# A macaron layer on one core: order of the opening's weight splits and the form of the last norm

## The chip, the cores and the metric

The kernel runs on one core of a Trainium2 chip. The metric is device microseconds of one execution; before, three runs took 982.69 to 983.95 us, median 983.18.

## What is computed

One residual layer on 512 tokens of width 1024, all in float32. `x` is normed, then three sub-layers follow, each of the form `x <- LayerNorm(ALPHA * x + w * gate * f(x * (1 + scale) + shift))`, with f a SwiGLU feed-forward net (D_FF = 2816), then a mixer (latent attention beside pooled channel groups), then a second SwiGLU net. Shift, scale and gate come from `silu(c) @ w_ada + b_ada`.

```python
x = _layernorm(x, ln_in_g, ln_in_b)
mod = (c_act @ w_ada[l] + b_ada[l]).reshape(B, N_SUBLAYERS, 3, D)
h = x * (1.0 + scale[:, 0, None, :]) + shift[:, 0, None, :]
y = _swiglu(h, ffn1_w_in[l], ffn1_w_out[l])
...
x = _layernorm(ALPHA * x + 0.5 * gate[:, 2, None, :] * y, post_ln_g[l, 2], post_ln_b[l, 2])

def _layernorm(x, g, b):
    mu = jnp.mean(xf, axis=-1, keepdims=True)
    var = jnp.mean(jnp.square(xf - mu), axis=-1, keepdims=True)
    return (xf - mu) * lax.rsqrt(var + LN_EPS) * g + b
```

## The kernel before

Activations are kept transposed: `x` is eight tiles (KD = 8) of 128 features by 512 tokens. A sum over features therefore runs over partitions and is made on TensorE with a matrix of ones. Weights come in units of 128x1024 (eight 128x128 blocks, one for each tile of h). For accuracy each factor is held as a high and a low part (`w_hi`, `w_lo`, `h_hi`, `h_lo`), and a product is three matmuls, w_hi with h_hi, w_hi with h_lo, w_lo with h_hi (`mm3`, L551 to L553). ScalarE writes a unit's high part (`act_hi`, L927), VectorE its low part (`dve_lo`, L935), from one of three slots `raw` that SyncE fills; the load of unit n waits until unit n - 3 is split (`s_lo`). Each engine runs its own hand-written program in order; semaphores join them.

**Opening.** SyncE loads the columns, x, c, and then in turn units and pairs of w_ada tiles (`ada_first`, a ring of 12). VectorE takes the input norm's statistics, and then for each k of 0 to 7: two products of w_ada with c (L1472) that give scale and shift of tile k (`first_columns`, L1475), the split of unit k while k < 6 (EARLY), and the low part of h of tile k - 1 (`first_low`, L1463). ScalarE normalises the token-major x (`normal`, L1051: four first halves ahead of the loop, the second halves in steps k = 0 and 1), TensorE transposes it back, ScalarE applies gain and offset (`affine`, L1056), makes h and its high part (L1069, L1072), and then splits unit k + 1. TensorE (`early_units`) fills six banks, one for each of units 0 to 5. In step k it adds the low part of tile k - 1 to the banks of units 0 to k - 1 (L614), catches up on unit k with all earlier tiles (L551 to L553), and adds the two high products of tile k to units 0 to k (L622, L623). Behind tile 7 it runs unit by unit from L627 on and then goes straight into the rest of the first net.

**Last norm.** TensorE closes the mean (L641, bank 6) and the mean square (L645, bank 7). ScalarE squares the mean (L945) and copies it (L946), VectorE forms the variance (L1262), ScalarE takes Ln (L950) and Exp (L952) of it, and VectorE refines that by one Newton step of three instructions (L1269, L1271, L1273). VectorE centres tiles 0 to 2 early, and then goes through the tiles in order, centring (L1276) and scaling (L1285). Gain and offset are applied by ScalarE (L1199; tiles 0, 2, 3, 5, 7) and GpSimd (L1771; tiles 1, 4, 6), and SyncE stores the tiles in order (L540), each behind its own wait.

## Time and profile before

| | |
|---|---|
| median of three runs | 983.18 us |
| the profiled execution | 983.47 us |
| its span, first to last instruction | 981.7 us |
| TensorE matmuls busy | 944.1 us, 96% |
| VectorE busy | 508.1 us, 52% |
| ScalarE busy | 373.2 us, 38% |
| GpSimd busy | 242.8 us, 25% |
| mean granted TensorE clock | 0.984 of full speed |
| moved by DMA | 127.20 MB, mean 130 GB/s |

Times within the trace are counted from the first instruction. In the page a slice is 24.5 us; all slices of TensorE but the first and the last show 90% or more. Engines are named PE (TensorE), DVE (VectorE), ACT (ScalarE), POOL (GpSimd) and SP (SyncE) in the rows; PEld are weight loads and SPq the DMA issues of SyncE. L12 is line 12 of the kernel.

### The profile page before, as it was taken

Reading aid. Unit: us, or ns where it says so; the run is one execution under the profiler, and the core shown is the slowest. Engines: PE = TensorE matmul, PEld = TensorE weight load, DVE = VectorE, ACT = ScalarE, POOL = GpSimd, SP = SyncE. Lnnn points to the kernel's source line nnn. Section 1 sums busy time; section 2 is a strip of 40 time slices with the busy share of each in tenths; the row PEclk is TensorE's granted clock in tenths of the full one; section 3 lists DMA queues with packets and bytes.
Section 4 is the critical chain, followed back from the end, with each engine's and each line's share of the span. In section 5 each row is a group of like instructions: output and inputs, shape, how many; then the busy total and the mean of one; then the engine's idle time right before and its main releaser. Section 6 shows DMA issues by size and latency. Waiting matters only on the chain.

```text
span 981.7 us, 10623 instructions
## 1 busy us (share of the span) xinstructions
PE 944.1 (96%) x4130; PEld 759.8 (77%) x4130; DVE 508.1 (52%) x718; ACT 373.2 (38%) x546; POOL 242.8 (25%) x209
## 2 busy tenths in 40 slices
PE   4999999999999999999999999999999999999992
PEld 3788888888888887787766786888888888888881
DVE  5956767454465764767655477722322232234225
ACT  4743232333222332765584447532333233222213
POOL 0021111111106221328934363611111111053110
PEclk8899999999999999999999999999999999999997
DMA  9836565656553753113501112223232323222202
GB/s 367 334 111 207 178 208 182 205 179 209 184 181 128 228 180 129 54 65 107 139 34 44 43 65 82 101 98 107 86 108 86 108 86 101 79 95 91 90 17 85
DMA packets 37474, 127.20 MB, mean 130 GB/s; under 512 B 4016, under 2 KB 4144, under 8 KB 37424
## 3 DMA queue, kind: packets, MB, share of 16 engines
q1 hardware_dynamic: 37424, 126.52, 38.4%
q8 instruction: 33, 0.54, 0.2%
q14 instruction: 17, 0.14, 0.0%
HBM read 123.36 MB, written 2.10 MB: 128 GB/s over the span
## 4 chain that ended last, share of the span: by engine, by line
PE 92%; DVE 3%; ACT 2%; issue 1%; POOL 1%; DMA 0%; SPq 0%; ACTq 0%; DVEq 0%; POOLq 0%
PE bank L551 28%; PE bank L553 28%; PE bank L552 28%; PE bank L856 2%; PE bank L833 1%; PE bank L659 1%; PE bank L623 1%; PE bank L622 1%; PE bank L614 1%; DVE x L1285 1%; DVE bn L1435 0%; PE bank L844 0%; PE bank L588 0%; DMA x<-xT 0%; POOL q_sum L1713 0%
## 5 line engine op out<-in xcount | busy, mean ns | idle before, releaser
L935 DVE TENSOR_TENSOR w_lo<-raw,w_hi 128x1024 fp32r<-128x1024 f32 x159 | 216.4, 1367 | 298.6 <-ACT w_hi L927 298.2
L551 PE MATMUL bank<-h_hi,w_hi 128*128 128x512 f32 x730 | 286.6, 393 | 0.0
L553 PE MATMUL bank<-h_hi,w_lo 128*128 128x512 f32 x730 | 284.4, 390 | 0.0
L552 PE MATMUL bank<-h_lo,w_hi 128*128 128x512 f32 x730 | 284.4, 390 | 0.0
L927 ACT ACTIVATE w_hi<-raw 128x1024 fp32r<-128x1024 f32 x159 | 162.3, 1032 | 204.0 <-PE bank L553 203.0
L1663 POOL TENSOR_TENSOR a_lo<-act_t,a_hi 128x512 fp32r<-128x512 f32 x44 | 58.4, 1328 | 426.7 <-ACT a_hi L1011 426.7
L551 PEld LDWEIGHTS bank<-h_hi,w_hi 128*128 128x128 f32 x730 | 137.3, 188 | 28.9 <-issue 0.8
L553 PEld LDWEIGHTS bank<-h_hi,w_lo 128*128 128x128 f32 x730 | 137.2, 188 | 29.0
L552 PEld LDWEIGHTS bank<-h_lo,w_hi 128*128 128x128 f32 x730 | 137.4, 188 | 28.6 <-issue 0.5
L551 PE MATMUL bank<-a_hi,w_hi 128*128 128x512 f32 x352 | 138.6, 394 | 0.0
L553 PE MATMUL bank<-a_hi,w_lo 128*128 128x512 f32 x352 | 137.0, 389 | 0.0
L552 PE MATMUL bank<-a_lo,w_hi 128*128 128x512 f32 x352 | 136.9, 389 | 0.0
L552 PEld LDWEIGHTS bank<-a_lo,w_hi 128*128 128x128 f32 x352 | 66.1, 188 | 14.7 <-issue 1.0
L551 PEld LDWEIGHTS bank<-a_hi,w_hi 128*128 128x128 f32 x352 | 66.1, 188 | 14.4 <-issue 1.0
L553 PEld LDWEIGHTS bank<-a_hi,w_lo 128*128 128x128 f32 x352 | 66.1, 188 | 13.8
L1217 DVE SCALAR_TENSOR_TENSOR var<-ada_ring,c_act 128x1024 bf16<-128x1024 f32 x56 | 72.5, 1296 | 3.6 <-DMA ada_ring<-ada_w 3.6
L1011 ACT ACTIVATE a_hi<-act_t 128x512 fp32r<-128x512 f32 x44 | 27.8, 632 | 110.0 <-DVE act_t L1325 103.3
L993 ACT ACTIVATE sq<-x 128x512 f32<-128x512 f32 x21 | 13.2, 628 | 108.3 <-DVE x L1313 108.2
L1313 DVE SCALAR_TENSOR_TENSOR x<-bank,gate,x 128x512 f32<-128x512 f32 x16 | 12.0, 750 | 77.3 <-PE bank L553 72.0
L1681 POOL TENSOR_TENSOR s_sum<-s_sum,x 128x512 f32<-128x512 f32 x15 | 23.0, 1534 | 98.1 <-DVE x L1313 93.9
L1020 ACT ACTIVATE act_t<-bank 128x512 f32<-128x512 f32 x42 | 25.0, 596 | 45.4 <-PE bank L553 45.4
L1672 POOL TENSOR_TENSOR x<-x,shift 128x512 f32<-128x512 f32 x16 | 25.9, 1654 | 57.6 <-DVE shift L1310 57.6
(252 smaller groups left out, 999.1 us busy)
## 6 DMA issues: line engine op xcount, KB each, us to landing
raw<-wunits SPq DMA_DIRECT2D x145, 512.0 KB, 3.2
ada_ring<-ada_w SPq DMA_DIRECT2D x56, 512.0 KB, 4.4
ada_first<-ada_w SPq DMA_DIRECT2D x16, 512.0 KB, 9.0
raw<-wunits SPq DMA_DIRECT2D x16, 384.0 KB, 2.8
x<-xT SPq DMA_DIRECT2D x4, 512.0 KB, 5.6
outT<-x SPq DMA_DIRECT2D x8, 256.0 KB, 2.0
K<-k_rope SPq DMA_DIRECT2D x2, 512.0 KB, 8.8
c_act<-c_rows SPq DMA_DIRECT2D x1, 512.0 KB, 7.5
```

Of the source, the lines that this page charges most:

```text
L551: mm(out, lh, rh, start=first, stop=False)
L552: mm(out, lh, rl, start=False, stop=False)
L553: return mm(out, ll, rh, start=False, stop=last)
L856: last = mm(bank[PV_BANK][:, j * P:], v, PT[hd % 2][:, j, j * P:], start=j == 0, stop=j == QB - 1)
L927: nc.scalar.activation(parts(n, 0, width)[0], raw[:, slot, 0:width], ACT.Copy)\
L935: nc.vector.tensor_tensor(lo, raw[:, slot, 0:width], hi.bitcast(F32), SUB).then_inc(s_lo, 1)
L1011: fn(a_hi[:, t - 1, :], act_t[:, (t - 1) % 2, :], ACT.Copy).then_inc(s_ah[f], 1)
L1020: fn(act_t[:, t % 2, :], bank[up_bank(f, t)][:], ACT.Silu).then_inc(s_silu[f], 1)
L1217: stt(junk, slot_ap, 1.0, c_act[:], MUL, MUL, accum_out=mod[:, t:t + 1])\
L1663: tt(a_lo[:, t, :], act_t[:, t % 2, :], a_hi[:, t, :].bitcast(F32), SUB)\
L1672: tt(x[:, m, :], x[:, m, :], shift[:], SUB).then_inc(s_xs[p], 1)
L1681: tt(s_sum[:], s_sum[:], x[:, m, :], ADD).then_inc(s_acc[p], 1)
```

## The change

In the opening each engine's split of a unit moves one step ahead: VectorE splits units 0 and 1 in step 0 and unit k + 1 in step k, and it does so behind `first_low(k - 1)`, no longer ahead of it. ScalarE splits unit 1 between the first four `normal` passes and the first `affine`, and unit k + 2 in step k. TensorE starts with two banks for tile 0 and catches up on unit k + 1 in step k; for unit 2's bank it waits for two second-half `normal` passes. SyncE issues units 1 and 2 right behind the first pair of w_ada tiles, and units 3, 4 and 5, each with its wait for a split, behind the pairs of steps 1, 2 and 3.

In the last norm the inverse root is one function of ScalarE, `Abs_reciprocal_sqrt`, read straight from the bank of the variance and loaded ahead of time by `preload`; the Newton step stays, with banks 0 and 1 as scratch. The tiles are centred on three engines: tile 0 on VectorE, tiles 1 to 3 on GpSimd by adding `shift` = -mean, tiles 4 to 7 on TensorE as an identity matmul of x plus one of `shift` into banks 2 to 5. VectorE scales seven tiles, GpSimd tile 3. ScalarE applies gain and offset to four tiles, GpSimd to three, VectorE to tile 7. The stores follow the new order.

```diff
@@ -74,7 +74,12 @@
 AFFINE_STEP = 4
-POOL_LAST = (1, 4, 6)
+LAST_POOL = (1, 2, 3)
+LAST_PE = (4, 5, 6, 7)
+LAST_SCALED = (4, 5, 0, 1, 2, 6, 7)
+LAST_ACT_OUT = (4, 5, 0, 2)
+LAST_POOL_OUT = (1, 6)
+LAST_STORED = (4, 5, 3, 0, 1, 2, 6, 7)
@@ -321,6 +326,7 @@
         def y_bank(p, m):
             return bank[OUT_BANK[m] if p == 2 else Y0 + m % 2]
+        ROOT_BANK, CENTRED_BANK = (0, 1), (2, 3, 4, 5)
@@ -411,6 +417,7 @@
         s_pf, s_mc = sem("pool_finished"), sem("mean_copied")
+        s_pc = sem("centred_by_matmul")
@@ -494,16 +501,16 @@
             for k in range(KD):
-                if k < RAWS:
-                    unit(k)
+                if k == 0:
+                    unit(0)
...
                         .then_inc(s_ada1[a % FIRST_RING], 16)
-                if RAWS <= k < EARLY:
-                    unit(k)
+                for n in range(1, RAWS) if k == 0 else range(k + 2, min(k + 3, EARLY)):
+                    unit(n)
@@ -532,11 +539,15 @@
                 unit(n)
-            for m in range(KD):
-                if m in POOL_LAST:
-                    sp.wait_ge(s_pf, POOL_LAST.index(m) + 1)
+            for m in LAST_STORED:
+                if m in LAST_ACT_OUT:
+                    sp.wait_ge(s_hh[3], LAST_ACT_OUT.index(m) + 1)
+                elif m == LAST_POOL[-1]:
+                    sp.wait_ge(s_pf, len(LAST_POOL) + 2)
+                elif m in LAST_POOL_OUT:
+                    sp.wait_ge(s_pf, len(LAST_POOL) + 3 + LAST_POOL_OUT.index(m))
                 else:
-                    sp.wait_ge(s_hh[3], m + 1 - sum(n < m for n in POOL_LAST))
+                    sp.wait_ge(s_nx[3], len(LAST_SCALED) + 1)
@@ -610,14 +621,18 @@
                         pe.wait_ge(s_hl[0], k)
-                        for j in range(min(k, EARLY)):
+                        for j in range(min(k + 1, EARLY)):
                             mm(bank[j][:], w(j, (k - 1) * P)[0], h_lo[:, k - 1, :], start=False, stop=False)
-                    if k < EARLY:
-                        pe.wait_ge(s_lo, k + 1)
+                    if k == 1:
+                        pe.wait_ge(s_xna, QB + 2)
+                    if 0 < k < EARLY - 1:
+                        pe.wait_ge(s_lo, k + 2)
                         for kk in range(k):
-                            mm3(bank[k][:], w(k, kk * P), h(kk), kk == 0, False)
+                            mm3(bank[k + 1][:], w(k + 1, kk * P), h(kk), kk == 0, False)
                     pe.wait_ge(s_hh[0], k + 1)
-                    for j in range(min(k + 1, EARLY)):
+                    for j in range(min(k + 2, EARLY)):
+                        if k == 0:
+                            pe.wait_ge(s_lo, j + 1)
@@ -715,6 +730,14 @@
                     down_tile(base, per, p, rhs, k_last, m, ready)
+            def last_centred():
+                pe.wait_ge(s_mc, 3)
+                for b, m in zip(CENTRED_BANK, LAST_PE):
+                    if m != LAST_PE[0]:
+                        mm(bank[b][:], ident, x[:, m, :], start=True, stop=False)
+                    mm(bank[b][:], ident, shift[:], start=False, stop=True).then_inc(s_pc, 1)
             def ffn(base, f, p, a_hi, a_lo):
@@ -732,7 +755,9 @@
                 if f == 1:
+                    mm(bank[CENTRED_BANK[0]][:], ident, x[:, LAST_PE[0], :], start=True, stop=False)
                     stats_end(p + 1)
+                    last_centred()
@@ -951,6 +976,16 @@
                 fn(y0[:], y0[:], ACT.Exp, scale=-0.5).then_inc(s_rq[p], 1)
+            def last_root():
+                act.wait_ge(s_st[3], 1)
+                fn(tmp[:], bank[MEAN[3]][:], ACT.Square).then_inc(s_rq[3], 1)
+                fn(shift[:], bank[MEAN[3]][:], ACT.Copy, scale=-1.0).then_inc(s_mc, 1)
+                act.wait_ge(s_rv[3], 1)
+                fn(y0[:], bank[SQR[3]][:], ACT.Abs_reciprocal_sqrt).then_inc(s_rq[3], 1)
+                act.wait_ge(s_rv[3], 4)
+                fn(bank[SQR[3]][:], rstd[:], ACT.Copy).then_inc(s_rq[3], 1)
             def preload(n, func):
@@ -1037,11 +1072,14 @@
                             act_hi(act, n)
-                preload(2 + f, ACT.Ln)
+                preload(2 + f, ACT.Abs_reciprocal_sqrt if f else ACT.Ln)
...
                 square(p, KD - 1)
-                root(p, 1, MX + LEAD if f == 0 else None)
+                if f == 0:
+                    root(p, 1, MX + LEAD)
+                else:
+                    last_root()
@@ -1059,6 +1097,7 @@
                 normal(t, 0)
+            act_hi(act, 1)
@@ -1070,8 +1109,8 @@
                 fn(h_hi[:, k, :], act_t[:, k % 2, :], ACT.Copy).then_inc(s_hh[0], 1)
-                if k + 1 < EARLY:
-                    act_hi(act, k + 1)
+                if k + 2 < EARLY:
+                    act_hi(act, k + 2)
@@ -1192,10 +1231,8 @@
             ffn(F2, 1, 3, a_hi2)
-            for m in range(KD):
-                if m in POOL_LAST:
-                    continue
-                act.wait_ge(s_nx[3], m + 1)
+            for m in LAST_ACT_OUT:
+                act.wait_ge(s_nx[3], LAST_SCALED.index(m) + 1)
@@ -1271,6 +1308,40 @@
                 stt(bank[SQR[p]][:], tmp[:], 1.5, y0[:], ADD, MUL).then_inc(s_rv[p], 1)
+            def last_norm():
+                mean, square = bank[MEAN[3]], bank[SQR[3]]
+                z, w = (bank[b] for b in ROOT_BANK)
+                dve.wait_ge(s_st[3], 2)
+                dve.wait_ge(s_rq[3], 1)
+                stt(square[:], square[:], SUM_EPS, tmp[:], ADD, SUB).then_inc(s_rv[3], 1)
+                dve.wait_ge(s_mc, 3)
+                centre(3, 0, mean)
+                dve.wait_ge(s_rv[3], 1)
+                dve.wait_ge(s_rq[3], 2)
+                tt(z[:], square[:], y0[:], MUL).then_inc(s_rv[3], 1)
+                dve.wait_ge(s_rv[3], 2)
+                stt(w[:], z[:], -0.5, y0[:], MUL, MUL).then_inc(s_rv[3], 1)
+                dve.wait_ge(s_rv[3], 3)
+                stt(rstd[:], w[:], 1.5, y0[:], ADD, MUL).then_inc(s_rv[3], 1)
+                dve.wait_ge(s_rv[3], 4)
+                for m in LAST_SCALED:
+                    if m == 0:
+                        dve.wait_ge(s_cen[3], 1)
+                        dve.wait_ge(s_rq[3], 3)
+                        scaled = tt(x[:, m, :], x[:, m, :], square[:], MUL)
+                    elif m in LAST_POOL:
+                        dve.wait_ge(s_pf, LAST_POOL.index(m) + 1)
+                        scaled = tt(x[:, m, :], x[:, m, :], square[:], MUL)
+                    else:
+                        dve.wait_ge(s_pc, LAST_PE.index(m) + 1)
+                        scaled = tt(x[:, m, :], bank[CENTRED_BANK[LAST_PE.index(m)]][:], rstd[:], MUL)
+                    scaled.then_inc(s_nx[3], 1)
+                m, c = LAST_SCALED[-1], 3 * KD + LAST_SCALED[-1]
+                dve.wait_ge(s_nx[3], len(LAST_SCALED))
+                ts(x[:, m, :], x[:, m, :], cols[:, C_LNG + c:C_LNG + c + 1],
+                   cols[:, C_LNB + c:C_LNB + c + 1], MUL, ADD).then_inc(s_nx[3], 1)
             def centre(p, m, mean):
@@ -1425,8 +1496,11 @@
                     plain_low(p, KD - 1)
-                root(p, 2, MX + LEAD if f == 0 else None)
-                normalise(p, MX if f == 0 else None)
+                if f == 0:
+                    root(p, 2, MX + LEAD)
+                    normalise(p, MX)
+                else:
+                    last_norm()
@@ -1473,10 +1547,10 @@
                 tt(first_col[:, k, :], mod_pair[:, k, :], bias_pair[:, k, :], ADD).then_inc(s_fc, 1)
-                if k < EARLY:
-                    dve_lo(dve, k)
...
                     first_low(k - 1)
+                for n in range(2) if k == 0 else range(k + 1, min(k + 2, EARLY)):
+                    dve_lo(dve, n)
@@ -1765,9 +1839,19 @@
             ffn(1, 3, a_hi2, a_lo2)
-            for m in POOL_LAST:
+            pool.wait_ge(s_mc, 3)
+            for m in LAST_POOL:
+                tt(x[:, m, :], x[:, m, :], shift[:], ADD).then_inc(s_pf, 1)
+            pool.wait_ge(s_pf, len(LAST_POOL))
+            pool.wait_ge(s_rv[3], 4)
+            m = LAST_POOL[-1]
+            tt(x[:, m, :], x[:, m, :], rstd[:], MUL).then_inc(s_pf, 1)
+            for m in (LAST_POOL[-1], *LAST_POOL_OUT):
                 c = 3 * KD + m
-                pool.wait_ge(s_nx[3], m + 1)
+                if m == LAST_POOL[-1]:
+                    pool.wait_ge(s_pf, len(LAST_POOL) + 1)
+                else:
+                    pool.wait_ge(s_nx[3], LAST_SCALED.index(m) + 1)
```

## Rows read from the trace of the kernel before

**Rows 1.** The page, part 1: busy us (share of the span) x instructions.

```profile
PE 944.1 (96%) x4130; PEld 759.8 (77%) x4130; DVE 508.1 (52%) x718; ACT 373.2 (38%) x546; POOL 242.8 (25%) x209
```

**Rows 2.** The chain of waits, 20 to 34: start us, us, what.

```profile
25.65 0.69 DVE h_lo L1463
27.18 0.43 PE bank L551
32.81 0.23 PE bank L553
```

**Rows 3.** Timeline of TensorE, end of the early units: start us, us, what.

```profile
63.38 0.39 PE L553 MATMUL bank<-h_hi,w_lo_early 128*128 128x512 f32 x1
```

**Rows 4.** Windows: length, busy us of each engine, granted clock, DMA share, GB/s.

```profile
24.00:26.00 2.00, 0.86 (x2) 0.14 (x1) 1.50 (x2) 2.00 (x4) 0.00 (x0) 0.50 1.01 414
32.00:33.00 1.00, 1.00 (x5) 0.81 (x4) 0.96 (x3) 1.00 (x2) 0.00 (x0) 0.77 0.89 320
```

**Rows 5.** The chain of waits, 960 to the end.

```profile
963.54 0.87 PE bank L645 x2
964.44 0.70 DVE var L1262
965.16 0.63 ACT y L950
965.81 1.28 ACT L952
967.11 0.64 ACT y L952
969.96 1.88 DVE x L1285 x3
978.48 0.81 ACT x L1199
```

**Rows 6.** Timelines of VectorE, ScalarE and TensorE in the opening.

```profile
19.03 1.22 DVE L935 TENSOR_TENSOR w_lo<-raw,w_hi 128x1024 fp32r<-128x1024 f32 x1
24.50 1.22 DVE L935 TENSOR_TENSOR w_lo<-raw,w_hi 128x1024 fp32r<-128x1024 f32 x1 [1.77 <-ACT w_hi L927]
28.81 1.23 DVE L935 TENSOR_TENSOR w_lo<-raw,w_hi 128x1024 fp32r<-128x1024 f32 x1
20.53 1.63 ACT L1056 ACTIVATE x<-bank,cols 128x512 f32<-128x512 f32 x2 [1.21 <-PE bank L588]
23.43 1.04 ACT L927 ACTIVATE w_hi<-raw 128x1024 fp32r<-128x1024 f32 x1
27.20 0.63 ACT L1072 ACTIVATE h_hi<-act_t 128x512 fp32r<-128x512 f32 x1
28.69 1.43 ACT L1051 ACTIVATE x_tok<-bank,tshift,trstd 128x512 f32<-128x512 f32 x2
26.39 0.80 PE L614 MATMUL bank<-h_lo,w_hi 128*128 128x512 f32 x1 [1.52 <-DVE h_lo L1463]
```

**Rows 7.** SyncE's timeline; DMA issues of 0:9.6, of 25:28 (count, KB, us to landing).

```profile
20.28 0.33 SPq L488 DMA_DIRECT2D raw<-wunits  x1
20.65 0.91 SPq L503 DMA_DIRECT2D ada_first<-ada_w  x2
ada_first<-ada_w SPq DMA_DIRECT2D x8, 512.0 KB, 12.2
raw<-wunits SPq DMA_DIRECT2D x1, 512.0 KB, 3.7
```

**Rows 8.** Timelines of TensorE and of SyncE at the end.

```profile
962.42 1.12 PE L641 MATMUL bank<-x,ones_d 128*128 128x512 f32 x2 [0.84 <-DVE x L1313]
979.32 0.33 SPq L540 DMA_DIRECT2D outT<-x  x1
```

**Rows 9.** GpSimd: L1672 by itself (ns min/median/max); L1771 among the groups.

```profile
L1672 POOL TENSOR_TENSOR x<-x,shift x16: 1290/1298/2271, 302.1 to 882.3; 128x512 f32<-128x512 f32 x16
L1771 POOL TENSOR_SCALAR x<-x,cols 128x512 f32<-128x512 f32 x3 | 2.3, 768 | 27.4 <-DVE x L1285 27.4
```

## The prediction

> **What bounds the kernel now.** I read the page's busy shares first: TensorE works 944.1 of 981.7 us [rows 1], so all that an edit can save outside TensorE's own work is in the 37.6 us in which it waits, and the chain of waits says where those are. Two stretches matter. In the opening TensorE stands still until the first low part of h (the `first_low` of tile 0, VectorE) is there at 26.34, and from 26.39 on it has no gap up to the last product of the early units, which ends at 63.77 [rows 2, 3]. It also starts that stretch at the lower clock: the granted clock is 0.50 in 24 to 26 and reaches 1.00 at about 32.5 (0.77 as a mean of 32 to 33) [rows 4], after work that had run unbroken since 26.39, and the step from one product to the next falls from 0.43 to 0.23 us [rows 2]. At the end TensorE is done at 964.4 and the last 17.3 us are a chain that it has no part in: variance, Ln, table load, Exp, three Newton steps, 13 passes over 128x512 on VectorE, one affine pass on ScalarE, one store [rows 5].
>
> **The opening, part by part.** In the order of before, unit 1 is split only behind h of tile 0: ScalarE makes `w_hi` of it at 23.43, VectorE waits 1.77 us for that, splits from 24.50, and only then comes `first_low(0)` at 25.65, for which TensorE waits 1.52 us [rows 6]. The change puts ScalarE's part (`act_hi(1)`, 1.04 us) into the idle 1.21 us ahead of the first affine pass at 20.53 [rows 6], so it costs ScalarE nothing; the cover is thin (0.17 us), and what it lacks shifts h of tile 0 by that much. VectorE's part follows unit 0 directly: 19.03 + 1.14 = 20.17, then to 21.3, with its operand ready at about 20.3. `first_low(0)` then stands behind two products of w_ada (2.3 us) alone and ends at about 24.4 instead of 26.3, and each later step of VectorE, whose period is 4.31 us (24.50 to 28.81) [rows 6], is some 0.8 to 1.9 us earlier.
>
> TensorE gets two banks' work for tile 0 (4 products instead of 2) from 23.67, at 0.43 us each to 25.5; then 2 low products to 26.4, 3 products that begin bank 2 (their `w_lo` is there at 25.6, the new wait for `s_xna` QB + 2 is over at 25.7, when the pair of normal passes ahead of the affine pass ends) to 27.7, and it meets h of tile 1 at 27.75, which ScalarE makes no earlier than before (27.20 + 0.53) [rows 6]. So it works on with about 0.1 us idle from 23.67. The number of products is the same 144 (6 units x 8 tiles x 3). Two prices bound the gain. If the clock rises when it did (32.5), before had 14 products done and after has 18: 4 x 0.23 = 0.9 us. If it rises up to 3 us earlier, as the unbroken work now begins 2.7 us earlier, the next hold is the wait for the second halves of x_tok at 30.0 (ScalarE 28.69 + 1.33 [rows 6], unchanged). There 15 products are done and 129 x 0.23 = 29.3 us are left, with four groups of transposes, each counted as two products (1.8): end 61.1. The same count for before from 32.5, 130 products and three groups, ends at 63.4. Gain 2.3. I take 1.9, nearer to the second end, since in before 6.1 us of unbroken work were enough, and 23.67 + 6.1 = 29.8. Later gates don't hold: `first_low(1)` at about 28.7, unit 3's `w_lo` at 29.9 and h of tile 2 at 32.05 stand against TensorE's need at 30.5, 31.2 and 32.6.
>
> SyncE's queue pays for this. Before, eight w_ada tiles were issued without a wait and unit 3 behind them at 20.28 [rows 7]. Now unit 3's wait for the first split (over at 20.2) stands ahead of tiles 4 to 15, and units 4 and 5 wait there too (21.3 and 25.6). The loads ahead of it, 6.4 MB, are in by about 18.4 at 414 GB/s [rows 4], so the DMA engines are idle for some 3 us that they were busy before. VectorE wants tiles 4 and 5 at 25.6 and 26.7. Issued at 20.7 and 21.1 into an empty queue and behind unit 3, with 3.7 us for a landing in 25 to 28 [rows 7] and 1.26 us more for each 0.52 MB, they land at about 24.7 and 26.0: 0.7 us of slack. Tiles 6 and 7 have 1.2. A miss of up to 1 us is taken up by the slack that TensorE's gates above show. Cost 0, bounds 0 to 1.
>
> **The end, part by part.** TensorE gets seven identity products behind the sums. The first (x of tile 4) lies in the 0.84 us in which it waits for the last residual; an f32 product takes 0.87 [rows 5, 8], so it may cost 0.1. The others begin when -mean is in `shift`, about 964.65, and give tiles 4, 5, 6 and 7 at 965.8, 967.5, 969.2 and 971.0 in banks, if the clock holds at 2.4 GHz. The variance stays as it is, 964.44 to 965.14. Then one ScalarE function for the root instead of Ln 0.63, load 1.28 and Exp 0.63 [rows 5]: the result is there at 965.8, not 967.75, 1.95 us saved. The three Newton steps have the same count and operands of the same kind: 965.8 + 3 x 0.73 = 968.0.
>
> Now VectorE has one centring pass (in the shade of the root), seven scalings and one affine pass, where it had five centrings and eight scalings from 969.96 to 978.45, 8.5 us. Scalings without a dependence follow each other at 0.60 (1.88 for three) [rows 5]: 968.0 + 6 x 0.6 + 0.7 = 972.3; the affine pass of tile 7 on VectorE has no row of its own shape here between 0.4 and 0.7 us (a pass from one SBUF tile against one from two); I take 0.5: 972.8. GpSimd: three centrings at 1.29 (its fastest and its middle row; 2.27 the slowest [rows 9]) from 964.7 to 968.5, scaling of tile 3 to 969.9, three affine passes at 0.77: tile 3 to 970.7, tile 1 (scaled at 970.4) to 971.5, tile 6 (scaled at 971.7) to 972.5. ScalarE: four affine passes of 0.81, the last (tile 2) to 971.9. The stores go out in the order 4, 5, 3, 0, 1, 2, 6, 7, each 0.33; the last at 972.95 in place of 979.32 [rows 8], and it takes 2.4 us to the end as now. End 975.3 against 981.7: 6.4 saved, less 0.1 for the product before the sums and 0.1 for stores that now follow each other closer. I take 6.2; the bounds are 5.2 (each hand-over 0.1 late, stores in a queue) and 6.6.
>
> **A rule on the load and one on the port.** The load of the table takes 1.28 us in the chain, and Exp begins 1.30 us after it began [rows 5]. The Trainium skill, ScalarE: Activation LUTs, section What ACT_TABLE_LOAD costs, gives 1.28 us and some 1.38 of draining on top, 2.66 in all; by that the end would save 1.4 us more. The trace has no such time between load and Exp, so the sum stays with 1.28. GpSimd's passes over x take 1.29 to 2.27 us [rows 9]; the long ones lie beside VectorE's splits, which read two SBUF tiles. The Trainium skill, SBUF — State Buffer, Reading the diagram, says that VectorE with two SBUF inputs or in a two-port mode and GpSimd lock each other out for whole instructions. All passes of VectorE in the new norm but the last take one operand from a bank, so by that rule 1.29 holds.
>
> **Sum.** 1.9 + 6.2 = 8.1. The profiled execution took 983.47 (span 981.7 and 1.8 around it): 975.4. It was 0.3 above the median of the three runs, 983.18, which would give 975.1; I say 975.2.
>
> **Rivals.** (1) Clock unchanged or loads late: TensorE keeps 1.2 GHz to 32.5, or waits about 1 us for w_ada tiles 4 and 5. For it: the gap at 24.86 was not the only thing ahead of the rise, and the slack of 0.7 us rests on a landing time in another load. Opening 0.9: 976.1. (2) GpSimd is slowed at the end. Its seven passes at 2.27 for those over two tiles: centrings end at 971.5, scaling 973.8, then three times 0.77 to 976.1, and the last store leaves at 976.8: the end saves 2.5, time 978.8. For it: such rows exist; against it: 0.77 for its affine pass while VectorE was scaling from a bank without a pause [rows 9]. (3) The change doesn't do what it says: the root function or the Square and Copy around it still draw a table load in the chain, because the set preloaded doesn't hold them all. 1.28 each, one or two: 976.5 to 977.8. Against it: in before Ln had been preloaded too, `root` ran a Square and a Copy behind that, and no load stands between the variance and Ln [rows 5]. (4) Slower than before: the refill of w_ada. VectorE takes 13 us from tile 5's landing to the split of unit 5 (three steps of 4.31), and TensorE has about 19.6 us of work behind that, so the opening ends at landing + 32.6. It decides from a landing at 31.2, when the opening gains nothing; to eat the end's 6.2 us too and 2 us more it must land at 39.4, 18 us after its issue. The longest middle value of a landing here is 12.2, in a full queue [rows 7], which would give 65.9 for the opening and 979.1 in all.
>
> **How the numbers follow.** Forecast 0.66 (974.2 to 976.0), rival 1 0.15, rival 2 0.07, rival 3 0.08, rival 4 0.01, and 0.03 for what I don't see. 0.2% is 2.0 us, about what a measurement tells from no change. All but rival 4 and the unseen lie over 5 us below before: faster 0.97, same 0.02, slower 0.01. The range leaves out rival 2, part of rival 3 and the rest: 974.1 to 977.4.
>
> **What would show it.** Right: TensorE without a gap over 0.3 us from 23.7; the clock at 1.00 before 30.5; the last early product ending at about 61.5 to 62; no table load behind the sums; the rstd bank or tile ready at 968.0, counted from a variance at 964.4; VectorE's last pass at about 8.4 us behind the variance; the span's end 10.9 us behind it (17.3 now). Wrong: VectorE waiting for ada_first over 1 us, GpSimd passes of 2 us in the last norm, stores that land over 3 us after issue, or a gap of TensorE between 64 and 962 that before didn't have.

## The result and the profile after

Four runs of the changed kernel took 976.36 to 978.24 us, median 976.99; four of the kernel before 982.69 to 984.07, median 983.57. The ratio is 0.9936 with a 95% interval of 0.9918 to 0.9953: 6.6 us faster, inside the range of the prediction, 1.8 us above its single value of 975.2. The profiled execution took 977.08 us, 6.4 less than that of before. Further down, each ratio is to runs of the kernel before that were made alongside, with medians of 983.55 to 984.01 us.

The page of the changed kernel: span, busy shares, and the granted clock in 40 slices.

```profile
span 975.3 us, 10654 instructions
PE 949.1 (97%) x4146; PEld 760.3 (78%) x4146; DVE 504.5 (52%) x711; ACT 370.7 (38%) x544; POOL 246.8 (25%) x213
PEclk8999999999999999999999999999999999999999
```

I cut both spans at two points, the start of the last early product and the start of the variance's instruction:

| | before | after | gain |
|---|---|---|---|
| first instruction to the last early product | 63.38 | 61.04 | 2.34 |
| from there to the variance (the middle) | 901.06 | 902.08 | -1.02 |
| variance to the end of the span (the tail) | 17.25 | 12.17 | 5.08 |
| span | 981.7 | 975.3 | 6.4 |

The opening, timelines of TensorE and then of VectorE (start us, us, what, idle before and its releaser), to be held against [rows 3, 6]:

```profile
23.46 0.50 PE L637 MATMUL bank<-h_hi,w_hi 128*128 128x512 f32 x1 [0.58 <-ACT h_hi L1111]
25.77 0.47 PE L562 MATMUL bank<-h_hi,w_hi 128*128 128x512 f32 x1 [0.49 <-ACT x_tok L1089]
27.77 0.50 PE L637 MATMUL bank<-h_hi,w_hi 128*128 128x512 f32 x1 [1.06 <-ACT h_hi L1111]
30.05 0.66 PE L599 MATMUL bank<-cols,x_tok 128*128 128x128 f32 x4 [0.63 <-ACT x_tok L1089]
61.04 0.39 PE L564 MATMUL bank<-h_hi,w_lo_early 128*128 128x512 f32 x1
23.81 0.68 DVE L1537 TENSOR_TENSOR h_lo<-act_t,h_hi 128x512 fp32r<-128x512 f32 x1
26.98 1.23 DVE L1546 SCALAR_TENSOR_TENSOR tmp<-ada_first,c_act 128x1024 bf16<-128x1024 f32 x1 [0.21 <-DMA ada_first<-ada_w]
```

`first_low(0)` starts at 23.81, no longer at 25.65, and TensorE has products of tile 0 up to 25.28. Behind them it waits three times: for a released bank (0.49), for h of tile 1 (1.06) and for the second halves of x_tok (0.63). The prediction had no gap over 0.3 us here. At the higher clock TensorE reaches these gates early; in the one profile of the new order in which the clock rose only at 26.8 the first two waits are missing. The granted clock stands behind them: as means of two windows, with busy times of PE, PEld, DVE, ACT and POOL, the clock, DMA share and GB/s, against 0.50 in 24 to 26 in [rows 4]:

```profile
20.00:24.00 4.00, 3.40 (x16) 2.57 (x15) 3.91 (x8) 3.63 (x6) 0.00 (x0) 0.70 0.72 256
24.00:26.00 2.00, 1.51 (x6) 0.74 (x5) 2.00 (x3) 2.00 (x4) 0.00 (x0) 1.00 0.92 291
```

It was up at 22.4, ten microseconds earlier than in before, while the 16 transposes of x_tok (19.25 to 22.9) still ran.

The end, from the chain of waits, to be held against [rows 5]:

```profile
963.12 0.71 DVE bank L1318
963.86 0.60 ACT y L985
964.56 0.71 DVE bank L1323
966.02 0.70 DVE rstd L1327
969.83 1.21 DVE x L1339 x2
971.06 0.55 DVE x L1343
```

One function of ScalarE stands between the variance and the Newton steps, with no table load. VectorE's last pass ends 8.5 us behind the start of the variance. GpSimd's part in its timeline: three centrings in 3.73 us, the scaling, two affine passes; the third affine pass follows at 970.53.

```profile
963.43 3.73 POOL L1844 TENSOR_TENSOR x<-x,shift 128x512 f32<-128x512 f32 x3 [16.46 <-ACT shift L983]
967.23 1.27 POOL L1848 TENSOR_TENSOR x<-x,rstd 128x512 f32<-128x512 f32 x1
968.61 1.52 POOL L1855 TENSOR_SCALAR x<-x,cols 128x512 f32<-128x512 f32 x2
```

### The profile page after: what moved, and what is told of

Same layout as the page of the kernel before. It is cut to its first block, busy times and chain, and to the rows that moved or that the text cites. A ratio compares the mean times of both kernels' runs of the same rounds, so it can differ in the third digit from the quotient of the medians.

```text
span 975.3 us, 10654 instructions
## 1 busy us (share of the span) xinstructions
PE 949.1 (97%) x4146; PEld 760.3 (78%) x4146; DVE 504.5 (52%) x711; ACT 370.7 (38%) x544; POOL 246.8 (25%) x213
## 4 chain that ended last, share of the span: by engine, by line
PE 91%; DVE 3%; ACT 3%; issue 1%; POOL 1%; DMA 1%; SPq 0%; ACTq 0%; DVEq 0%; POOLq 0%
PE bank L562 28%; PE bank L564 28%; PE bank L563 28%; PE bank L881 2%; PE bank L858 1%; PE bank L674 1%; PE bank L637 1%; PE bank L638 1%; DMA x<-xT 1%; PE bank L625 1%; ACT x_tok L1089 1%; PE bank L869 1%; DVE bn L1509 1%; DVE w_lo L960 0%; POOL q_sum L1787 0%
```

## Where the middle lost one microsecond

Matching TensorE's instructions of both traces one by one shows the same lead of 2.34 us from the opening up to 481 us, and of 1.3 us from 491 on; nothing changes after that. The place is the start of the attention, a place that the change doesn't touch. VectorE's and GpSimd's timelines of before:

```profile
487.29 1.23 DVE L935 TENSOR_TENSOR w_lo<-raw,w_hi 128x1024 fp32r<-128x1024 f32 x1
487.36 2.29 POOL L1749 TENSOR_TENSOR h_lo<-act_t,h_hi 128x512 fp32r<-128x512 f32 x1
```

and of after, with TensorE's instruction behind it:

```profile
485.06 2.36 DVE L960 TENSOR_TENSOR w_lo<-raw,w_hi 128x1024 fp32r<-128x1024 f32 x1
485.05 1.29 POOL L1823 TENSOR_TENSOR h_lo<-act_t,h_hi 128x512 fp32r<-128x512 f32 x1
489.13 0.70 PE L858 MATMUL bank<-K,Q 128*128 128x256 f32 x2 [0.66 <-ACT cq L1193]
```

The weight split on VectorE reads two SBUF tiles, and so does GpSimd's pass over h. In before the split started 0.07 us ahead and took 1.23 us, and GpSimd's pass took 2.29, stretched by the split. In after GpSimd's pass started 0.01 us ahead and kept its 1.29, and the split took 2.36. The split stands in VectorE's queue ahead of the next score's maximum, so ScalarE's exponential and TensorE's next scores come late. The Trainium skill, SBUF — State Buffer, Reading the diagram, states that the one of the two that starts first holds the shared port for its whole instruction; these four rows agree: the first keeps its time, and the second ends 1.14 us (before) and 1.08 us (after) behind the end of the first, 0.15 less than it takes by itself. My prediction used that rule for the last norm and not for what the whole shift of the timeline does to ties elsewhere.

## Experiments

**The opening alone.** The five pieces of the diff in SyncE's loop over k, `early_units`, ScalarE's and VectorE's opening; the last norm is that of before.

```diff
             for t in range(QB):
                 normal(t, 0)
+            act_hi(act, 1)
...
-                if k < EARLY:
-                    dve_lo(dve, k)
                 if k:
                     first_low(k - 1)
+                for n in range(2) if k == 0 else range(k + 1, min(k + 2, EARLY)):
+                    dve_lo(dve, n)
```

> Only the opening's part of the change; the last norm is that of before. My theory: the opening gives 2.3 us of TensorE's time, of which about 0.8 are the products drawn ahead and up to 1.5 the earlier rise of the clock, and of what it gives some 1 us can be lost again at the start of the attention steps, where a split on VectorE and a GpSimd pass start within 0.1 us of each other. Time 1.3 to 2.3 us below before, ratio 0.9977 to 0.9987; last early product at 61.0 to 62.4 of the span. Rival (the clock does it all): nothing where the clock rises as late as in before (32.5), and the last early product not before 63.

Measured: 981.62 us, ratio 0.9975 (0.9965 to 0.9986). Last early product at 61.17, middle 902.04, tail 17.25. The opening gives its 2.2 us and the middle takes 1.0 back with the last norm untouched: the loss belongs to the opening's part. The ratio lies just outside the range expected, and the profiled execution (982.25) was the slowest of seven. In this profile VectorE waited 1.37 us for w_ada tile 5, the sign of a late refill that the prediction had named; TensorE's other gates hid all but 0.2 us of it.

**The last norm alone.** The rest of the diff.

```diff
-                root(p, 2, MX + LEAD if f == 0 else None)
-                normalise(p, MX if f == 0 else None)
+                if f == 0:
+                    root(p, 2, MX + LEAD)
+                    normalise(p, MX)
+                else:
+                    last_norm()
```

> Only the last norm's part of the change; the opening is that of before. My theory: from the variance to the span's end 12.2 us as in the changed kernel, not 17.3, so 5.1 us below before, ratio about 0.9948, and nothing lost in the middle. Rival (the two parts disturb each other, the 1.0 us lost in the middle belongs to the norm's part): 4.1 us.

Measured: 979.61 us, ratio 0.9951 (0.9939 to 0.9964), tail 12.16, middle 901.05. The two parts don't disturb each other.

**The split first.** The changed kernel with the order of the two passes fixed.

```diff
                 if step in low_after:
+                    if step == 1:
+                        pool.wait_ge(s_lo, S_FILL + LEAD + 1)
                     pool_low(low_after[step])
```

> The changed kernel with one more wait: GpSimd's second pool_low (step 1 of the attention) waits until VectorE has split the unit of step 2, so that the split always comes first, as it did in the profile of before. If the 1.0 us lost in the middle is that race, TensorE starts the third score product of head 2's group without the stall of 0.66 us, the middle (from the last early product to the variance) has the same length as in before, 899.3 instead of 900.3 us, and the time is 1.0 us below the changed kernel: 975.9 to 976.2. If the loss has another cause (transfers that now meet, the clock) it stays at 977.0.

Measured: 976.23 us, ratio 0.9923 (0.9909 to 0.9936), last early product 61.03, middle 901.10, tail 12.18. (The two lengths of the middle in the expectation are 1.8 us too small, both; their difference is what was at stake.) VectorE's and GpSimd's rows:

```profile
484.96 1.23 DVE L960 TENSOR_TENSOR w_lo<-raw,w_hi 128x1024 fp32r<-128x1024 f32 x1
486.27 1.29 POOL L1823 TENSOR_TENSOR h_lo<-act_t,h_hi 128x512 fp32r<-128x512 f32 x1 [1.17 <-DVE w_lo L960]
```

**GpSimd first, in the kernel before.** The other direction.

```diff
+                if step == 2:
+                    dve.wait_ge(s_pl, 2)
                 if step % 6 == 2:
                     lo_after(S_FILL + step // 6)
```

> The kernel before with one more wait: VectorE's split at step 2 of the attention waits until GpSimd's second pool_low is done, the order that the changed kernel fell into. If that order is the cause of the 1.0 us lost in the middle, the middle (last early product to variance) grows from 901.1 to about 902.1 to 902.3 us and the time rises by 1.0 to 1.2 us over before (ratio 1.0010 to 1.0013). If the loss had another cause it stays at 901.1.

Measured: 984.70 us, ratio 1.0008 (0.9999 to 1.0017); middle 902.36, 1.30 longer than in before. By the run times alone this would be unclear; the trace shows it at the place:

```profile
487.08 1.29 POOL L1751 TENSOR_TENSOR h_lo<-act_t,h_hi 128x512 fp32r<-128x512 f32 x1
488.40 1.23 DVE L935 TENSOR_TENSOR w_lo<-raw,w_hi 128x1024 fp32r<-128x1024 f32 x1 [1.47 <-POOL h_lo L1751]
```

Counted from the last early product, since this profile's opening ended 0.36 us ahead of before's, the split ends 1.47 us later than in before; in the changed kernel it was 1.24 later. Most of the 0.3 us over the 1.0 of the lost tie is thus the wait itself: the split starts only 0.03 us behind the end of GpSimd's pass and then takes its full 1.23. So the cause of the middle's loss is shown from both sides. Over all profiles the middle is 901.0 to 901.2 where the split starts first and 902.0 to 902.4 where it doesn't. With the new opening and nothing done about the order it came second in five of seven profiles, with starts 0.02 us apart or less, and first in two, by 0.09 and 0.11; with the old one first in all four, by 0.07 to 0.13. Which way it goes is the luck of one execution.

**More transposes ahead of the changed opening.** TensorE repeats 32 of the transposes of x between the statistics and the token-major norm, into the same banks.

```diff
+WARM = 2
...
+                pe.wait_ge(s_bn, BN_PARTS * QB)
+                for i in range(WARM):
+                    for k in range(KD // 2, KD):
+                        for t in range(QB):
+                            nc.tensor.transpose(bank[TOKEN_BANK[1][t]][:, k % 4 * P:(k % 4 + 1) * P],
+                                                x[:, k, t * P:(t + 1) * P], ident)
                 pe.wait_ge(s_xna, QB)
```

> The changed kernel with 32 more transposes (a repeat of those of x into the same banks) on TensorE between the statistics and the token-major norm, in time in which it waits. If the opening is held by the wait for the second halves of x_tok at 30.0 once the clock is up, an earlier rise gives nothing more: last early product at 61.0 to 61.5, time as the changed kernel's within 0.5 us, and the runs spread less. Rival (the clock still costs in most runs): up to 1 us below the changed kernel.

Measured: 975.90 us, ratio 0.9917 (0.9903 to 0.9930), last early product 61.52, middle 901.10 (the tie won), tail 12.18. The median is 1.1 us below the changed kernel's. The profiled execution is 0.5 below: the middle gives 1.0 and the opening takes 0.5, so the transposes didn't speed the opening up. The clock rose at 26.8 here, and this profile shows the refill of w_ada at its worst. Its chain of waits has the landing of tile 5 and VectorE's product behind it:

```profile
20.99 7.38 DMA ada_first<-ada_w
28.39 1.25 DVE tmp L1553 x2
```

VectorE wanted that tile at 26.8 and got it at 28.4, a wait of 1.62 us; in the changed kernel's profile it waited 0.21. From TensorE's wait for the second halves of x_tok to the last early product it takes 32.00 us here and 30.99 in the changed kernel.

**The same transposes ahead of the old opening.**

```diff
+WARM = 2
...
+                pe.wait_ge(s_bn, BN_PARTS * QB)
+                for i in range(WARM):
...
                 pe.wait_ge(s_xna, QB)
```

> The kernel before with 32 more transposes on TensorE between the statistics and the token-major norm, no other edit. It prices the clock alone. My theory: where the clock then rises ahead of 30, TensorE in the old order is held by the same wait for x_tok's second halves at 30.0 with 10 products done and ends its early units at about 62.2 to 62.5, 1.3 us ahead of before: time 1.0 to 1.5 us below before (ratio 0.9985 to 0.9990). Rival (the order is worth all of the 2.3 us): the end of the early units stays at 63.4 to 63.8 whatever the clock does, time as before.

Measured: 983.07 us, ratio 0.9996 (0.9987 to 1.0005); last early product 62.69. Of the 0.69 us against before 0.41 are an earlier start: the first product with h of tile 0 stands at 23.26 and not at 23.67. The expectation missed: the clock didn't stay up. TensorE's wait for `first_low(0)`, and two windows behind it:

```profile
25.98 0.50 PE L621 MATMUL bank<-h_lo,w_hi 128*128 128x512 f32 x1 [2.02 <-DVE h_lo L1470]
26.00:28.00 2.00, 1.69 (x6) 1.12 (x7) 2.00 (x3) 1.97 (x4) 0.00 (x0) 0.97 1.01 414
28.00:30.00 2.00, 1.48 (x4) 0.67 (x4) 1.96 (x5) 2.00 (x4) 0.00 (x0) 0.50 1.04 420
```

The clock was at 2.4 GHz from 17.6 on, TensorE stood still for 2.0 us, worked 1.7 us of the next 2, and the clock fell to 1.2 GHz at 27.9 until 31.3.

**The gap filled as well.** The last kernel with eight products in the gap, into a bank that is overwritten later.

```diff
...
+                    if k == 1:
+                        for i in range(8):
+                            mm(bank[1][:], w(0, 0)[0], h_hi[:, 0, :], start=True, stop=True)
                     if k:
                         pe.wait_ge(s_hl[0], k)
```

> The old order with 32 more transposes ahead of the opening and, in the gap in which TensorE waits for the first low part of h, eight products whose result is overwritten. So the clock should stay at 2.4 GHz through the gap, where with the transposes alone it fell again at 27.9. It prices the order apart from the clock. If the old order with a full clock is held by the wait for x_tok's second halves at 30.0 with 10 products done instead of 15, the last early product starts at about 62.0 to 62.2 (the changed kernel 61.0, before 63.4): order 1.0, clock 1.3 of the 2.3. Rival (the clock was all): 61.0 to 61.3.

Measured: 982.98 us, ratio 0.9993 (0.9984 to 1.0002); last early product 63.12. TensorE's rows, `first_low(2)` on VectorE and a window (granted clock 1.00, as from 18 on without a break):

```profile
26.41 0.50 PE L624 MATMUL bank<-h_lo,w_hi 128*128 128x512 f32 x1 [0.16 <-DVE h_lo L1473]
30.20 0.66 PE L589 MATMUL bank<-cols,x_tok 128*128 128x128 f32 x4 [1.09 <-ACT x_tok L1061]
35.05 0.96 PE L624 MATMUL bank<-h_lo,w_hi 128*128 128x512 f32 x3 [0.41 <-DVE h_lo L1473]
34.31 0.68 DVE L1473 TENSOR_TENSOR h_lo<-act_t,h_hi 128x512 fp32r<-128x512 f32 x1
63.12 0.39 PE L554 MATMUL bank<-h_hi,w_lo_early 128*128 128x512 f32 x1
24.00:28.00 4.00, 3.52 (x15) 2.26 (x13) 3.47 (x5) 3.97 (x7) 0.00 (x0) 1.00 1.02 416
```

The same two rows in before:

```profile
35.32 0.95 PE L614 MATMUL bank<-h_lo,w_hi 128*128 128x512 f32 x3
34.27 0.69 DVE L1463 TENSOR_TENSOR h_lo<-act_t,h_hi 128x512 fp32r<-128x512 f32 x1
```

This is the miss from which I learned most. With the old order and a full clock the opening ends 0.26 us earlier than before and not 1.3. TensorE gains 1.1 us, waits them for x_tok (1.09), and then meets the next bound, the end of `first_low(2)` at 34.99, for which it waits 0.41 us. From 35.05 it has 120 products and two groups of transposes: 120 x 0.227 + 0.9 = 28.1, which gives 63.2. That is VectorE's chain: two products of w_ada, a split, a low part, 4.3 us a step, without a pause. In before TensorE reached the same point at 35.32, 0.36 us behind the end of `first_low(2)` (34.96), so the low clock cost nearly nothing there. The kernel with the transposes alone says the same: counted from its first product with h of tile 0, the last early product comes after 39.44 us, here after 39.43 and in before after 39.72, though the clock was low there from 27.9 to 31.3 and here not at all. The new order starts VectorE's chain earlier (`first_low(2)` at 32.55), and only that lets TensorE use its clock.

**Loads as before.** The changed kernel with SyncE's old order.

```diff
-                if k == 0:
-                    unit(0)
+                if k < RAWS:
+                    unit(k)
...
-                for n in range(1, RAWS) if k == 0 else range(k + 2, min(k + 3, EARLY)):
-                    unit(n)
+                if RAWS <= k < EARLY:
+                    unit(k)
```

> The changed kernel with SyncE's order of loads as in before. It prices the refill. In the changed kernel VectorE waits 0.2 us for w_ada tile 5 and TensorE is held elsewhere, so by my theory the order of the loads is worth nothing: last early product at 60.9 to 61.5, time that of the changed kernel within 0.5 us. Rival (units 3 to 5 now come later behind a full queue and hold ScalarE's splits): end of the early units 0.5 to 1.5 us later.

Measured: 976.51 us, ratio 0.9924 (0.9909 to 0.9940), last early product 60.86, middle 902.15, tail 12.18. VectorE no longer waits for tile 5:

```profile
26.49 1.22 DVE L1546 SCALAR_TENSOR_TENSOR tmp<-ada_first,c_act 128x1024 bf16<-128x1024 f32 x1
```

The new order of the loads gives nothing in the opening: from the first product with h of tile 0 to the last early product it takes 37.59 us in both kernels, and the 0.18 us between them is an earlier start. The new order only brings the risk: of eight profiles with it seven show a wait of VectorE for tile 5, from 0.16 to 1.62 us.

**Half the bytes in the stores.** The second 256 tokens of every output tile are left out.

```diff
-                sp.dma_start(outT[m], x[:, m, :]).then_inc(s_out, 16)
+                sp.dma_start(outT[m][:, 0:TOK // 2], x[:, m, 0:TOK // 2]).then_inc(s_out, 16)
```

> The changed kernel, but each store writes only the first 256 of its tile's 512 tokens; the other half of the output is left out. The same eight issues, half the bytes. If the eight stores that now follow each other at the DMA engines' rate set the end (2.1 MB from 969.0 to 974.5), the way from the variance to the end falls from 12.2 to about 10.9 to 11.1 us. If the time of VectorE's last pass or a store's fixed time sets it, it falls by no more than 0.3 (half of one tile's transfer).

Measured: 975.52 us, ratio 0.9917 (0.9901 to 0.9934); tail 10.98, 1.19 less than in the changed kernel. The DMA view of a window of 10 us, rate in 40 slices of a quarter microsecond and the median time from issue to landing, first of the changed kernel from 965.3 on:

```profile
GB/s 0 0 0 0 0 0 0 0 0 0 0 0 0 0 0 188 401 410 303 401 418 410 393 402 401 410 402 401 410 418 410 410 401 402 402 393 205 0 0 0
outT<-x SPq DMA_DIRECT2D x8, 256.0 KB, 2.5
```

then with half the bytes, from 965 on:

```profile
GB/s 0 0 0 0 0 0 0 0 0 0 0 0 0 0 0 33 373 119 115 369 168 365 160 361 156 365 144 369 160 369 156 369 49 0 0 0 0 0 0 0
outT<-x SPq DMA_DIRECT2D x8, 128.0 KB, 1.8
```

In the changed kernel the engines move 400 GB/s from 969.3 to 974.5 with no pause; with half the bytes they pause after each store.

**The last store from ScalarE.**

```diff
-                sp.dma_start(outT[m], x[:, m, :]).then_inc(s_out, 16)
+                if m != LAST_STORED[-1]:
+                    sp.dma_start(outT[m], x[:, m, :]).then_inc(s_out, 16)
...
+            act.wait_ge(s_nx[3], len(LAST_SCALED) + 1)
+            nc.scalar.dma_start(outT[LAST_STORED[-1]], x[:, LAST_STORED[-1], :]).then_inc(s_out, 16)
```

> The changed kernel with the last store (tile 7) issued by ScalarE, which is free by then, not by SyncE. If SyncE's issues (about 0.5 us each when they follow each other) set the end, the store leaves 0.4 us earlier and the end comes 0.4 us earlier. If the DMA engines' rate does, the end stays within 0.15 us, 12.1 to 12.3 us behind the variance.

Measured: 977.18 us, ratio 0.9933 (0.9919 to 0.9948); tail 12.22. The store leaves at 972.01, 8.52 us behind the variance and not 8.78 as in the changed kernel. It buys nothing, since the store takes 3.2 us to land and not 3.0:

```profile
outT<-x SPq DMA_DIRECT2D x7, 256.0 KB, 2.4
outT<-x ACTq DMA_DIRECT2D x1, 256.0 KB, 3.2
```

So it is the rate, not SyncE's issues and not the last pass, that sets the end.

**Ln and Exp in the new norm.**

```diff
-                fn(y0[:], bank[SQR[3]][:], ACT.Abs_reciprocal_sqrt).then_inc(s_rq[3], 1)
+                fn(y0[:], bank[SQR[3]][:], ACT.Ln).then_inc(s_rq[3], 1)
+                act.wait_ge(s_rq[3], 2)
+                fn(y0[:], y0[:], ACT.Exp, scale=-0.5).then_inc(s_rq[3], 1)
...
-                preload(2 + f, ACT.Abs_reciprocal_sqrt if f else ACT.Ln)
+                preload(2 + f, ACT.Ln)
...
```

> The changed kernel with Ln and Exp in place of the one root function; all else as changed. It prices the root by itself. Everything behind the root shifts by the table load and one function: 1.28 + 0.63 + 0.04 = 1.95 us, so from the variance to the end 14.1 us, and the time 1.9 to 2.0 us above the changed kernel. Rival (the stores' rate hides part of it): tiles centred on TensorE and GpSimd are ready earlier than the root, the stores come out closer, and only 1.2 to 1.6 us show.

Measured: 978.90 us, ratio 0.9952 (0.9937 to 0.9967), tail 14.10, 1.93 longer. ScalarE's timeline:

```profile
963.23 0.60 ACT L985 ACTIVATE y<-bank 128x512 f32<-128x512 f32 x1 [0.51 <-DVE bank L1320]
963.84 1.28 ACT L987 ACT_TABLE_LOAD   x1
965.14 0.63 ACT L987 ACTIVATE y<-y 128x512 f32<-128x512 f32 x1
968.06 0.60 ACT L989 ACTIVATE bank<-rstd 128x512 f32<-128x512 f32 x1 [2.29 <-DVE rstd L1329]
```

The load takes 1.28 us and Exp begins 1.30 behind its start, in this position too. Of the 5.08 us of the tail 1.93 are the root's and 3.15 the spreading of the passes. The stores' rate hides none of it: every store moves with the root.

**Together.** The changed kernel with the transposes, the split first, and tile 4 scaled, finished and stored in two halves.

```diff
...
+                    if m == LAST_SCALED[0]:
+                        dve.wait_ge(s_pc, 1)
+                        src = bank[CENTRED_BANK[0]]
+                        tt(x[:, m, 0:half], src[:, 0:half], rstd[:, 0:half], MUL).then_inc(s_nx[3], 1)
+                        scaled = tt(x[:, m, half:TOK], src[:, half:TOK], rstd[:, half:TOK], MUL)
...
```

> The changed kernel with three additions: the 32 transposes ahead of the opening, the split of step 2 ahead of GpSimd's pool_low, and tile 4, the first to be stored, scaled, finished and stored in two halves, so that the stores start about 0.5 us earlier. Early units end at 61.0 to 61.5, middle 901.1, and 11.7 to 11.9 us from the variance to the end, if the stores' rate sets the end. Time 975.2 to 975.7, ratio to before about 0.991. If the last tile's passes set the end, the halves give nothing and cost up to 0.3: 12.2 to 12.5 us behind the variance.

Measured: 976.31 us, ratio 0.9925 (0.9912 to 0.9937); last early product 61.05, middle 901.21, tail 12.23. The halves give nothing. The rates from 964.5 on show why:

```profile
GB/s 0 0 0 0 0 0 0 0 0 0 0 0 0 127 365 148 365 45 279 393 410 402 401 393 401 418 393 410 418 410 426 393 393 402 393 426 180 0 0 0
```

Counted from the variance, the first half leaves 0.42 us earlier (4.78 and not 5.20), but the engines then run dry twice: the next two stores follow 0.49 and 0.71 us later, while 128 KB are moved in 0.33 us at 400 GB/s. VectorE's last pass ends 0.06 us later, since its two half passes take 0.68 us together and the whole one took 0.60. The intervals of this kernel, of the one with the transposes, of the one with the split first and of the changed kernel overlap; I can't call any of them faster than the change.

## Why the prediction was right, and where it was off

**Right: the opening's size.** 1.9 us forecast, 2.34 measured, and the hold that I took as the upper end, x_tok's second halves at 30.0, is there at 30.05. The wait for tile 5 was 0.21 us where I had 0.7 us of slack; the landing came at 26.98, not at 26.0. The reason for which I chose 1.9, that 6.1 us of unbroken work had been ahead of the rise in before, did not carry over: in after the clock was up before the first product of tile 0, 3.1 us into the transposes.

**Half right: the opening's cause.** I priced the lead at 0.9 us at the old clock and at 2.3 with the earlier rise, so that 1.4 would be the clock's. With the clock held up in the old order the gain is 0.26 us; the old opening was held by VectorE's chain as well, 0.36 us behind which TensorE ran. At a full clock the new order is worth 2.1 us (63.12 against 61.04, and 61.05 in the kernel of the last experiment, whose clock was up from 17.5). What it is worth at the old clock, Rival 1's 0.9, was met in no profile, so the 2.34 can't be divided further. Without added transposes the clock rose between 22.3 and 24.0 in all seven profiles with the new order, and at 31.5 to 32.4 in the three with the old one. In two of the seven it rose at 23.9, behind the transposes, and the opening was as long as in the others (37.6 us from the first product with h of tile 0). Why it rises ten microseconds earlier in the one case I can't say: TensorE was busy for 3.64 us in 20 to 24 in before and for 3.40 in after. The old gap alone can't be it, since it comes later than 22.4. It stays open.

**Not foreseen: the middle.** I had it at nothing, and named a gap between 64 and 962 only as a sign of being wrong. 1.02 us, from a tie for the port that two passes win or lose by a hundredth of a microsecond. Whether it is lost is luck: in two of seven profiles of the new opening the split still came first.

**Mis-sized: the end.** 6.2 us forecast, 5.08 measured. The chain came as worked out: root 1.93 us (1.95), VectorE's last pass at 8.5 us behind the variance (8.4), GpSimd at 1.24 to 1.27 a pass, no table load. The term that failed is "0.1 for stores that now follow each other closer". From the end of VectorE's last pass, 971.61, to the end of the span it takes 3.68 us, where my terms had 2.5 and this 0.1. Eight tiles of 256 KB are 2.1 MB, and at the 400 GB/s that the opening's windows show too [rows 4] they take 5.2 us. The first is issued at 968.3 and its bytes move from 969.3 on, so the last can't be in before 974.5. I had spread the stores at the pace at which tiles came ready, one in 0.55 us on average, and hadn't divided the bytes by the rate.

**The sum.** 2.34 - 1.02 + 5.08 = 6.40, against 1.9 + 6.2 = 8.1. The middle (-1.02) and the end (-1.12) fell short by 2.1 us together, and the opening gave 0.44 back, so the forecast is nearer than its parts, which is luck. Two of my signs of being wrong came true, a gap of TensorE between 64 and 962 (0.66 us at 489) and, in two other profiles, a wait of over 1 us for w_ada. And one reading was wrong when I wrote it: rival 2's 978.8 lies 4.4 us below before, not over 5. Rival 2 (GpSimd slowed in the last norm) didn't come, but the same port, elsewhere, cost a microsecond. Rival 3 didn't come. Rival 4's mechanism is real and small: waits of 1.37 and 1.62 us in two profiles, which made the way from the wait for x_tok to the last early product 0.2 and 1.0 us longer.

## What to carry to other kernels

When a change speeds a stretch up, divide the bytes that leave behind it by the rate of the DMA engines: once work is faster than that, the first store's time and the bytes set the end. When it shifts everything behind it, look for places where VectorE and GpSimd both start a pass over SBUF tiles within a tenth of a microsecond; if one of them is on the path, fix the order with a wait. And before the clock is blamed for a slow start, ask what the engine would have waited for at full clock: here that was a moment 0.3 us earlier.

## What the runs showed of the hardware that I had not expected

A granted clock of 2.4 GHz was lost by one pause: with 2.0 us of stillness at 24 to 26 and 1.7 us of work in 26 to 28 it fell at 27.9; with the pause filled by eight products it stayed. A store of 256 KB lands in 2.0 us by itself, as in before, and in up to 3.0 when eight follow each other, as in the changed kernel, at about 400 GB/s in both cases while it moves. Of two passes that want the shared port the loser's time is what is left of the winner's plus its own less 0.15 (1.23 becomes 2.36, 1.29 becomes 2.29), and in one profile the split started 0.006 us ahead by the records and still lost.

The clock also rose inside a run of nothing but transposes. In the kernel before with added transposes, the run in TensorE's timeline, and three windows:

```profile
13.88 5.38 PE L608 MATMUL bank<-cols,x 128*128 128x128 f32 x32 [2.26 <-DVE bn L1442]
14.00:16.00 2.00, 2.00 (x12) 2.00 (x13) 1.66 (x13) 0.00 (x0) 0.00 (x0) 0.56 1.02 416
17.00:18.00 1.00, 1.00 (x8) 1.00 (x7) 1.00 (x3) 1.00 (x2) 0.00 (x0) 0.68 1.01 414
18.00:20.00 2.00, 1.65 (x16) 1.42 (x15) 1.97 (x4) 1.55 (x3) 0.00 (x0) 1.00 1.04 426
```

TensorE had been idle for 2.26 us, and the clock fell to 1.2 GHz at 14.2. After it stand 32 transposes of 128x128 in fp32 without a pause, from 13.88 to 19.26, and from 17.6, in the middle of them, it was at 2.4 GHz. The Trainium skill, TensorE: Matmul & The Clock Gate, Part 4: PE-mode transpose, says that the full clock doesn't engage for transpose mode. The trace doesn't name the mode of these instructions; for `nc.tensor.transpose` on fp32 it shows, as does the rise at 22.4 in the changed kernel, that the clock rises while nothing else runs on TensorE.
